# Two token tiles' expert rows made by TensorE and ScalarE instead of GpSimd

## What is computed

```python
def modulate(x, g, shift, scale):      # shift and scale: one row for latent, one for context tokens
    return rms_norm(x, g) * (1 + scale) + shift

def hier_moe(h, wg, bg, we, be, w_gate, w_up, w_down):
    g_logits = h @ wg + bg                               # router, on h
    ...                                                  # one group, two of its experts, weights
    for g in range(MOE_GROUPS):
        a, u = h @ w_gate[g], h @ w_up[g]                # experts, on h
        out = out + (silu(a) * u * combine) @ w_down[g]
```

## Time and profile before

| | |
|---|---|
| median of 3 runs | 1999.48 us (1996.73 to 2000.74) |
| the profiled execution | 2006.07 us |
| its span, first to last instruction | 2004.3 us |
| mean granted TensorE clock | 0.985 |
| PE, DVE, ACT, POOL busy | 95%, 61%, 32%, 13% of the span |
| DMA, mean over the span | 162 GB/s |

### The profile page before, as it was taken

How to read it: one execution, slowest core, us unless ns; L and a number is a source line. 1 busy time by engine, 2 the same in 40 slices (tenths; PEclk the granted TensorE clock), 3 DMA queues, 4 the chain that set the end, 5 groups by cost and what they waited for, 6 DMA issues and landing times.

```text
span 2004.3 us, 29470 instructions
## 1 busy us (share of the span) xinstructions
PE 1902.1 (95%) x11126; PEld 1076.7 (54%) x11126; DVE 1222.8 (61%) x1967; ACT 641.2 (32%) x1274; POOL 266.8 (13%) x322
## 2 busy tenths in 40 slices
PE   7999999999999999999998999889998999998997
PEld 4866875544444444555645764533335678645332
DVE  3212777487787664368854643667766657447776
ACT  2001762200000001242313640356653556323542
POOL 3000110011111000012200002711102000051101
PEclk9989999999999999999999999999998999999999
DMA  8632100677677343410110102689966020139995
GB/s 264 168 84 85 53 13 22 210 252 254 224 249 261 123 175 113 144 43 28 57 43 27 59 5 83 267 331 341 364 263 235 1 85 2 36 122 364 390 418 209
DMA packets 108763, 323.97 MB, mean 162 GB/s; under 512 B 9160, under 2 KB 43240, under 8 KB 90193
## 3 DMA queue, kind: packets, MB, share of 16 engines
q1 hardware_dynamic: 78112, 190.63, 26.5%
q0 software_dynamic: 25264, 112.79, 15.7%
q10 hardware_dynamic: 5248, 18.68, 2.3%
HBM read 291.55 MB, written 35.76 MB: 163 GB/s over the span
## 4 chain that ended last, share of the span: by engine, by line
PE 80%; DVE 6%; DMA 5%; issue 4%; PEld 2%; PEldq 2%; ACT 1%; DVEq 0%; POOL 0%; ACTq 0%; SPq 0%; POOLq 0%
PE ps L3702 15%; PE ps L3061 7%; PE ps L467 7%; PE ps L2217 6%; PE ps L1190 5%; PE ps L1236 4%; PE ps L3501 4%; PE ps L1211 4%; PE ps L365 3%; PE ps L3082 3%; PE ps L1837 3%; DMA X<-moe_rows,row_token 3%; PE ps L336 2%; PE ps L1915 2%; PE ps L2193 2%
## 5 line engine op out<-in xcount | busy, mean ns | idle before, releaser
L3702 PE MATMUL ps<-wide 128*128 128x512 f32 (+1 forms) x736 | 306.5, 575 | 1.9 <-issue 1.7
L3702 PEld LDWEIGHTS ps<-wide 128*128 128x128 f32 x736 | 138.3, 190 | 166.2 <-issue 164.1
L3061 PE MATMUL ps<-wide,X 128*32 x448 | 197.5, 594 | 2.1 <-DVE X L3240 2.1
L3061 PE MATMUL ps<-Z,X 128*32 128x512 f32 x1344 | 197.9, 594 | 0.0
L2217 PE MATMUL ps<-wide 128*128 128x512 f32 (+1 forms) x384 | 148.3, 542 | 0.5 <-issue 0.5
L1544 DVE SCALAR_TENSOR_TENSOR Z<-Z,wide 128x2048 f32<-128x2048 f32 x56 | 131.6, 2350 | 2.8
L1190 PE MATMUL ps<-T 64*128 64x256 f32 (+1 forms) x888 | 110.3, 378 | 9.7 <-DVE nm L1329 6.4
L3061 PEld LDWEIGHTS ps<-wide,X 128*32 128x32 f32 x448 | 47.0, 110 | 124.1 <-issue 124.1
L1261 ACT ACTIVATE T<-T,nm 128x768 f32<-128x768 f32 (+3 forms) x112 | 86.7, 775 | 76.2 <-DVE nm L1329 76.2
L2217 PEld LDWEIGHTS ps<-wide 128*128 128x128 f32 x384 | 71.6, 190 | 68.7 <-issue 65.3
L3737 ACT ACTIVATE Z<-ps 128x512 f32<-128x512 f32 x22 | 13.1, 597 | 289.8 <-PE ps L3702 289.7
(11 more groups left out here) (448 smaller groups left out, 3497.8 us busy)
## 6 DMA issues: line engine op xcount, KB each, us to landing
wide<-in_experts SPq DMA_DIRECT2D x64, 1024.0 KB, 8.5
Z<-in_mod_w POOLq DMA_DIRECT2D x32, 1024.0 KB, 5.2
T<-in_experts SPq DMA_DIRECT2D x32, 1024.0 KB, 11.8
X<-in_mod_w POOLq DMA_DIRECT2D x16, 1024.0 KB, 5.4
moe_out<-X ACTq DMA_DIRECT2D x25, 512.0 KB, 8.5
wide<-in_w_down SPq DMA_DIRECT2D x12, 1024.0 KB, 6.9
wide<-in_w_gate SPq DMA_DIRECT2D x22, 512.0 KB, 6.1
wide<-in_w_up SPq DMA_DIRECT2D x22, 512.0 KB, 7.0
```

The lines of the kernel that those rows point to most:

```text
L3061: last = pe.matmul(ps[rows, t % 2, :], mo.xT[:, c, rows], w_rows, start=(c == 0), stop=(c == DK - 1))
L3702: last = pe.matmul(self.gu.bank(u)[:, columns], w, self.rhs(c)[:, columns], start=(c == 0), stop=(c == DK - 1))
```

## The change

The last two tiles of the list (`i >= n - 2`: the context tiles in the first layer, tiles 2 and 3 in the second) get their rows in another way. POOL still spills them, but makes no row of them. PE turns them back out of `k.HT`, which already has gain and shift: four groups of four transposes into PSUM banks 5 and 6, where the 16 keep-awake matmuls stood, but ahead of the drain that raises `places_free`; the third and fourth group wait until ACT has copied the first and the second. ACT copies each group (128x512) to the row's place in SBUF, two behind the first exponential and two behind the second. POOL issues the two stores in `Router.gpsimd`, behind the wait for the spills and the gates' load, each when its two copies are done. With no context rows left for POOL, the second set of gain and shift, its two loads and DVE's instruction on it go.

```diff
-        self.sets = both[:len(mods)]
+        self.sets = both[:1]
@@ RowStores.gpsimd
             pool.dma_start(self.away[:, t, :], k.X[:, t, :]).then_inc(k.spilled.sem, 16)
+            if i >= self.n - 2:
+                continue
             for c in range(0, D, 256):
                 ch.step(pool.tensor_tensor(row[:, c:c + 256], self.norm.hn[:, t, c:c + 256], gain[:, c:c + 256], ALU.mult))
+    def turn(self, pe):
+        k = self.k
+        for u in range(4):
+            t = self.norm.tiles[self.n - 2 + u // 2]
+            if u >= 2:
+                pe.wait_ge(k.rows_copied.sem, self.copied + u - 1)
+            for j in range(4):
+                last = pe.transpose(k.ps[:, 5 + u % 2, j * P:(j + 1) * P], k.HT[:, 4 * (u % 2) + j, t * P:(t + 1) * P], k.ident[:, :])
+            last.then_inc(k.rows_turned.sem, 1)
+
+    def copy_turned(self, act, which):
+        k = self.k
+        for u in which:
+            act.wait_ge(k.rows_turned.sem, self.turned + u + 1)
+            row = self.place(self.n - 2 + u // 2)
+            act.activation(row[:, 512 * (u % 2):512 * (u % 2) + 512], k.ps[:, 5 + u % 2, :], ACT.Copy).then_inc(k.rows_copied.sem, 1)
+
+    def store_turned(self, pool):
+        k = self.k
+        for i in range(self.n - 2, self.n):
+            t = self.norm.tiles[i]
+            pool.wait_ge(k.rows_copied.sem, self.copied + 2 * (i - self.n + 2) + 2)
+            pool.dma_start(self.rows_out[t * P:(t + 1) * P, :], self.place(i)).then_inc(k.rows_stored.sem, 16)
@@ Router.gpsimd
         for dst, src in self.rows_gate:
             pool.dma_start(dst, src).then_inc(k.small_landed.sem, 16)
+        self.stores.store_turned(pool)
         self.stores.await_rows(pool)
@@ Router.tensor
         self.banks.filled(last)
+        self.stores.turn(pe)
         pe.drain().then_inc(k.places_free.sem, 1)
-        keep_awake(pe, k, 7, 16)
@@ Router.scalar
             act.activation(to[:, 0:n, :], x[:, 0:n, :], ACT.Exp).then_inc(k.step_done.sem, 1)
+            self.stores.copy_turned(act, (2 * i, 2 * i + 1))
@@ the first layer's head
-        head = [Loading(k, gate_loads(0, 2, 2)), row_stores(0, even.then, 2), even.then]
+        head = [Loading(k, gate_loads(0, 2, 2)), row_stores(0, even.then, 1), even.then]
```

More of the change, by code:

```diff
@@ L2592, in __init__ @@
         self.stored, self.spilled = k.rows_stored.reserve(16 * n), k.spilled.reserve(16 * n)
+        self.turned, self.copied = k.rows_turned.reserve(4), k.rows_copied.reserve(4)
         self.n = n
@@ L2605, in gpsimd @@
         for i, t in enumerate(self.norm.tiles):
-            gain, shift = self.sets[0 if t < ST else 1]
+            gain, shift = self.sets[0]
             row = self.place(i)
@@ L3932, in two_blocks @@
         k.head_squares, k.head_roots, k.heads_normed = tally("head_squares"), tally("head_roots"), tally("heads_normed")
+        k.rows_turned, k.rows_copied = tally("rows_turned"), tally("rows_copied")
         k.both_done, k.next_tiles_back = tally("both_done"), tally("next_tiles_back")
```

## The result

The changed kernel takes **2004.1 us** (median of 21 runs) against 1999.48 us (21 runs): ratio 1.0022, with an interval of 1.0013 to 1.0031. The forecast was 1999.1 us and no measurable change; the time lies within the range given, but the change makes the kernel slower by 0.22%. The profiled execution takes 2008.57 us, 2.5 us more than that of before.

What follows compares the result with a forecast made beforehand. Bound by the router's DVE chain at the first layer's seam, by keep-awake blocks and the third gather at the second's. First layer -0.9 and second +0.5 gave -0.4 us: 1999.1 us, range 1995.5 to 2004.5.

Steps and rivals of the forecast that it cites:

- (1): At both seams, DVE's chain without POOL beside it gets shorter: 1.2 us in the first layer, 1.9 in the second.
- (2): PE's 16 transposes replacing 16 keep-awake matmuls at both seams stay hidden behind the wait for DVE's chain: cost 0.
- (5): ACT's two copies of 0.6 us fit between the exponentials: cost 0, at worst 0.3 us.
- (3): places_free and SP's two loads for expert 3 come 3.3 to 4 us later, hidden by queued DMA work: cost 0.
- (4): First layer's keep-awake block slows to 7.66 us, leaving 0.9 of 1.2 us saved; bounds 1.2 and minus 4.1.
- Rival 3: Clock stays at 1.2 GHz through the keep-awake block in both layers: +7.4 us, 2006.9 us; chance 0.06.
- (6): Row stores behind spills and gates' load: first layer 0; second layer's first gather 1.7 us late, costing 0.5 us.
- (7): Two loads and one DVE instruction fewer at the first layer's head, 1.2 us of DVE: worth 0.

Runs made afterwards that it cites:

- first layer alone: The change made in the first layer only, the second layer as in the kernel before; 1.0006 of the kernel before.
- stores first: The changed kernel with POOL issuing the two row stores ahead of its wait for the spills and the gates' load; 1.0008 of the kernel before.
- second layer alone: The change made in the second layer only, the first layer as in the kernel before; 1.0017 of the kernel before.
- twelve back: The changed kernel with 12 keep-awake matmuls put back, four between the turns and eight behind the drain; 0.9995 of the kernel before.
- late stores: Kernel before, POOL making all rows, last two stored behind spills' wait and gates' load; 1.003 both layers, 1.0012 second only, 0.9987 first only.

## Why the prediction was wrong

(1) *POOL makes two tiles fewer*: **right.** DVE's lines take 0.17 to 0.28 us at both seams:

```profile
1803.29 0.17 DVE L2775 SCALAR_TENSOR_TENSOR rO<-rG,rs 128x16 f32<-128x16 f32 x1 [0.15 <-DVE rG L2773]
...
1803.91 0.22 DVE L2779 TENSOR_TENSOR T<-rL,rO 128x64 f32<-128x64 f32 x1
```

In the first layer the gather goes 1.2 us sooner (104.5 after 105.65 us from the projection), in the second the keep-awake block starts 1.7 us sooner (forecast 1.9).

(2), (5) *Turns and copies*: **right**, hidden. PE still idles 2.8 us ahead of line 2830, waiting for DVE:

```profile
1291.33 0.71 PE L2830 MATMUL ps<-Z 128*128 128x96 f32 x2 [2.81 <-DVEq L2800]
```

(3) *Expert 3's loads later*: **right.** They go at 1805.20 (before 1801.87) and the DMA was full until about 1821.

(4) *PE's clock*: **one of the two steps that failed.** I charged it 0.3 us, for a longer keep-awake block, with its bound for that block, too. The block did stretch (7.5 us, 8.7 in the second profile). What I had not looked for is that the level could be down again behind it. In five of the six profiles in which the first layer lacks its 16 keep-awake matmuls (three of the change, first layer alone, matmuls removed) the first quad took 8.4 to 9.8 us against 7.07 before, and in the profiled execution it ran at 1.2 GHz with PE busy; the sixth, stores first, had 7.07. There a gather 1.2 us early becomes a first quad that ends 1.8 us late, and by the end of that layer's experts they are 3.1 us behind (of the last 1.3 us of this I know no cause). Over an execution it is 11 to 16 us of slow clock. Removing the matmuls alone brings that about (14.1 us), and twelve of them put back undo it (-0.1 us). In place of -0.9 us the first layer alone measured +1.2 [-1.2, 3.6], which by itself does not shut out the forecast. Rival 3 had this cause, at the wrong place and with too large a price. Chance has a part in it: two of the seven profiles that keep the 16 matmuls have a slow first quad and a third a slow second one, and none of the three with twelve. The Trainium skill (TensorE: Matmul & The Clock Gate, Part 4: PE-mode transpose), by which transposes are no such activity as matmuls, spoke against the change; the runs don't test it by itself, since leaving out the matmuls with no transposes in their place had the same effect.

(6) *Stores behind the spills*: **the time of the gather right, its price under-sized, and with it the other step that failed.** Forecast was a gather 30.1 us after SP's first load and a first use of the rows by PE 0.4 us late; measured are 30.3 and 0.5. Two small errors cancel in this: the last row landed at 30.0 us, not 29.5, and POOL went 0.3 us behind it, not 0.6. The down loads were to be 1.7 us late and are 2.7. From this I took 0.5 us, arguing that the third gather would now go ahead of them. That holds at the seam, where the second quad starts on time. In the change the price falls 30 us later, in a wait for weights, which I put down to the 1.1 MB that the DMA didn't move in the gap. Over all profiles, wherever the first gather goes 29.8 us or more behind SP's first load (change three times, second layer alone, twelve back, late stores in both layers and in the second) the sixth gather goes at 73.6 to 75.0 us, elsewhere at 69.5 to 71.3: 2.3 to 5.5 us against the forecast's 0.5. There are two ways to it. In the change and with the second layer alone, where the keep-awake block is long (8.6 to 9.1 us), the seam is on time and PE waits for weights later. With twelve back and late stores, where that block takes 6.47 us, PE stands still for the gather (4.5, 2.1 and 2.0 us), the first quad is slow, and the 3 us are lost at the seam. By time the second layer alone loses 3.4 us [1.0, 5.8], late stores there 2.4 us [-0.4, 5.0]; the 1.7 us by which the chain is shorter are lost in the wait for rows.

(6) in the first layer cost nothing that can be told: late stores there alone gave -2.6 us, for which I have no reason, and the gather waits for `row_token` in every profile of the change. (7) no run tests by itself.

**The sum** with measured terms: 1.2 us (first layer alone) and 3.4 us (second alone) make 4.6; the change measured 4.4. Forecast were -0.9 and +0.5. Both terms were too low by 2 to 3 us, through what happens after the place at which I stopped counting. How the 3.4 us of the second layer split between missing matmuls and late rows isn't shown: the matmuls alone, in both layers, cost 2.8 us and late stores alone, in this one, 2.4 us, and either interval takes in 0. What is shown is that undoing both takes the loss away.

**What stays open**: why twelve back, with its sixth gather as late as the change's, is no slower than before (the clock won back may hide it, but no run here separates them), why late stores in both layers cost more than the two parts, and how much of the slow-clock time is caused by the missing matmuls and how much by waits.

## What to carry to other kernels

Matmuls that only keep TensorE busy are priced by the work that comes after them: before one is taken away, look for the places behind it where the engine will idle next (here the first quad, some 25 us on), and count a possible fall to 1.2 GHz at each. A late transfer can be free where it lands and paid for later: where loads queue behind it, carry the bytes that the less busy DMA doesn't move into the next stretch with a full DMA, and look at the landings there. Filler kept in the gaps of the new work and each store issued as soon as its data are there turned +3.2 to +6.4 us into -1.6 and -3.4.

## What was not expected of the hardware

- The granted clock is 0.50 again at 1312 to 1314 us, with PE busy 2.00 of 2.00 us, after 1.00 at the end of the keep-awake block. It was still 1.00 while PE waited for the gather (1305.6 to 1307.65) and fell at 1308, when PE had just begun to turn the gathered rows. The kernel before has the same wait (1.90 us), and no fall there. The same program differs between executions in this, and so a single profile doesn't price it (first quad 8.5 to 9.3 us in three profiles of the change, keep-awake block 7.5 to 8.7 us).
- The second layer's keep-awake block takes 6.47 us with 4 matmuls in one gap and 8 behind, and 7.86 in the kernel before, with all 16 behind the drain. It isn't the place of the matmuls alone that decides this: late stores, with all 16 behind the drain, have 6.47 us as well. There the low level fell on the 16 (5.46 us instead of 3.83), with twelve back on the first quad.
- Two stores of 0.5 MB behind a load of 0.5 MB in POOL's queue take 12.3 and 14.9 us beside SP's loads (13.6 in the view is their median), with a DMA share of about 1.0 until 1821. The Trainium skill (DMA: Bandwidth & Descriptors, Queues, rings and completion order) tells of turns between the queues packet by packet; the trace doesn't show equal shares of bytes: 1.5 MB from the first issue at 1806.5 to the last landing at 1822.4 is 99 GB/s, a quarter of the 412 GB/s that all queues moved from 1808 to 1821.
